# Writing the low halves of streamed weights over the loaded unit: six shared slots in place of four double ones, and a ScalarE lead of four or five units

## The reference, cut to what matters

```python
def swiglu(h, w1, w3, w2):
    return (jax.nn.silu(h @ w1) * (h @ w3)) @ w2

def conv_glu_ffn(x, w_up, conv_w, conv_b, w_down):
    h = causal_depthwise_conv(x @ w_up, conv_w, conv_b)
    g, u = jnp.split(h, 2, axis=-1)
    return (jax.nn.silu(g) * u) @ w_down
```

## Time and profile before

| | us |
|---|---|
| median of 3 runs | 2924.38 |
| lowest and highest | 2919.39, 2924.88 |
| the profiled execution | 2921.18 |
| its span, first to last instruction | 2919.4 |
| TensorE busy in it | 2652.9 |
| GpSimd busy in it | 1870.5 |
| ScalarE, DVE busy in it | 1460.7, 1122.1 |
| loaded from memory | 418.52 MB, 144 GB/s over the span |

### The profile page before, as it was taken

The page is one execution under the profiler, slowest core; times in us unless marked ns, Lnnn a source line. Parts: engine busy times, 40 slices in busy tenths (PEclk is TensorE's granted clock), DMA queues, the critical chain, the costliest instruction groups (busy, mean ns, idle before and its releaser), DMA issues.

```text
span 2919.4 us, 53645 instructions
## 1 busy us (share of the span) xinstructions
PE 2652.9 (91%) x19652; PEld 2493.6 (85%) x19652; DVE 1122.1 (38%) x2614; ACT 1460.7 (50%) x2539; POOL 1870.5 (64%) x789
## 2 busy tenths in 40 slices
PE   4999889999989989998889978899898899888997
PEld 2887679999977789998889977799878799878997
DVE  3316644111145621225343365433433433463334
ACT  4326644434444544445555565555545555464555
POOL 6437646878855678873468855388635588535686
PEclk8999999999999999999999998999979999999999
DMA  6224434555533545542345533255423355423454
GB/s 241 92 80 159 145 109 138 186 165 185 183 126 134 173 158 180 188 152 76 101 150 179 192 118 120 89 181 180 146 79 116 109 184 181 133 73 116 147 180 135
DMA packets 115063, 421.75 MB, mean 144 GB/s; under 512 B 12768, under 2 KB 13792, under 8 KB 114400
## 3 DMA queue, kind: packets, MB, share of 16 engines
q1 hardware_dynamic: 114336, 413.39, 42.7%
q10 hardware_dynamic: 576, 6.23, 0.5%
HBM read 418.52 MB, written 1.05 MB: 144 GB/s over the span
## 4 chain that ended last, share of the span: by engine, by line
PE 46%; issue 30%; POOL 17%; DVE 3%; ACT 2%; POOLq 0%; DMA 0%; ACTq 0%; SPq 0%; DVEq 0%
POOL ring_low L2064 17%; PE bank L560 8%; PE bank L561 8%; PE bank L566 8%; PE bank L551 6%; PE bank L552 6%; PE bank L553 5%; PE bank L767 1%; ACT scr L1188 1%; PE bank L796 1%; PE bank L684 1%; ACT ring_high L1078 1%; DVE rstd L1544 1%; PE bank L681 0%; DVE scr L1523 0%
## 5 line engine op out<-in xcount | busy, mean ns | idle before, releaser
L2064 POOL TENSOR_TENSOR ring_low<-ring,ring_high 128x1024 fp32r<-128x1024 f32 x785 | 1870.3, 2405 | 1028.7 <-ACT ring_high L1078 702.9
L560 PE MATMUL bank<-high,ring_high 128*128 128x256 f32 (+1 forms) x3372 | 858.5, 290 | 20.8 <-ACT ring_high L1294 10.0
L561 PE MATMUL bank<-low,ring_high 128*128 128x256 f32 (+1 forms) x3372 | 850.8, 288 | 0.0
L560 PEld LDWEIGHTS bank<-high,ring_high 128*128 128x128 f32 x3372 | 648.2, 192 | 29.6 <-ACT ring_high L1294 11.4
L561 PEld LDWEIGHTS bank<-low,ring_high 128*128 128x128 f32 x3372 | 648.4, 192 | 6.4
L1294 ACT ACTIVATE ring_high<-ring 128x1024 fp32r<-128x1024 f32 x462 | 479.7, 1052 | 54.1 <-PE bank L560 34.3
L566 PE MATMUL bank<-high,ring_low 128*128 128x256 f32 (+1 forms) x3372 | 492.6, 288 | 2.3 <-POOL ring_low L2064 2.3
L566 PEld LDWEIGHTS bank<-high,ring_low 128*128 128x128 f32 x3372 | 445.5, 192 | 9.5 <-POOL ring_low L2064 3.9
L1078 ACT ACTIVATE ring_high<-ring 128x1024 fp32r<-128x1024 f32 x323 | 337.9, 1055 | 166.0 <-PE bank L560 55.4
L551 PE MATMUL bank<-hid_high,ring_high 128*128 128x256 f32 x1232 | 352.1, 286 | 12.0 <-POOL ring_low L2064 12.0
L552 PE MATMUL bank<-hid_low,ring_high 128*128 128x256 f32 x1232 | 351.4, 285 | 0.0
(11 more groups left out here) (201 smaller groups left out, 3447.0 us busy)
## 6 DMA issues: line engine op xcount, KB each, us to landing
ring<-in_units SPq DMA_DIRECT2D x785, 512.0 KB, 3.3
xt<-in_x ACTq DMA_DIRECT2D x1, 2048.0 KB, 14.3
nbias<-in_bias ACTq DMA_DIRECT2D x1, 1536.0 KB, 7.8
consts<-in_consts ACTq DMA_DIRECT2D x1, 1472.0 KB, 8.5
vt<-in_mem ACTq DMA_DIRECT2D x1, 1024.0 KB, 6.3
out_x<-xt SPq DMA_DIRECT2D x8, 128.0 KB, 1.7
cols<-in_cols SPq DMA_DIRECT2D x1, 711.0 KB, 8.3
```

The source lines that it names most:

```text
L560: first = pe.matmul(out, w[0], x[0], start=start, stop=False)
L561: pe.matmul(out, w[0], x[1], start=False, stop=False)
L2064: pool.tensor_tensor(whole(ring_low, u), whole(ring, u), whole(ring_high, u).bitcast(fp32), ALU.subtract).then_inc(unit_ready, 1)
```

## The change

The low half is written over the unit that was loaded: `ring_low` becomes a second name, with the rounded type, for the memory of `ring`. The memory that is freed gives both rings six slots, of two blocks each (raw or low, and high). A slot can now be loaded again only when TensorE has released it, so SP waits for `unit_used` of unit u - 6, and ScalarE needs no wait of its own for a release. Outside the feed-forward stages `feed(u)` still goes up to u + 3. A feed-forward stage begins with `feed(u0, 5)`: units 3 and 4 are rounded before tile 0, and each tile rounds 3n + 4, 3n + 5 and 3n + 6. The last tiles leave out what brings the lead back to three units for the next stage.

```diff
-RING = 4
+RING = 6
+AHEAD = 4
...
+        ring_at = nc.sbuf_base
         ring = sb("ring", RING * UNIT)
+        ring_low = nc.alloc_sbuf_tensor_at("ring_low", [P, RING * UNIT], fp32r, offset=ring_at)
         ring_high = sb("ring_high", RING * UNIT, fp32r)
-        ring_low = sb("ring_low", RING * UNIT, fp32r)
...
-                        sp.wait_ge(unit_ready, r * RING + (s + 1 - RING))
+                        sp.wait_ge(unit_used, r * RING + (s + 1 - RING))
...
-                def feed(u):
+                def feed(u, ahead=AHEAD):
-                    while fed[0] < min(u + RING, N_UNITS):
+                    while fed[0] < min(u + ahead, N_UNITS):
                         v = fed[0]
                         act.wait_ge(loaded[v % RING], 16 * (v // RING + 1))
-                        if v >= RING:
-                            act.wait_ge(unit_used, v - RING + 1)
                         act.activation(whole(ring_high, v), whole(ring, v), ACT.Copy).then_inc(unit_high, 1)
...
-                    assert fed[0] == u0 + RING - 1
-                    def tile(r, n):
+                    assert fed[0] == u0 + AHEAD - 1
+                    feed(u0, AHEAD + 1)
+                    def tile(r, n, fed_ahead=False):
...
-                                act.wait_ge(unit_used, r * (3 * BODY) + (u - RING + 1))
...
-                            feed_tile([3])
+                            if not fed_ahead:
+                                feed_tile([4])
...
-                        feed_tile([4])
+                        feed_tile([5])
...
-                        feed_tile([5])
+                        if n < FT - 1:
+                            feed_tile([6])
                     for n in range(2):
-                        tile(0, n)
+                        tile(0, n, fed_ahead=n == 0)
...
-                    fed[0] = u0 + 3 * FT + 3
+                    fed[0] = u0 + 3 * FT + AHEAD - 1
```

More of the change, by code:

```diff
@@ L521, in _ @@
                 for u in range(rounds * RING, N_UNITS):
-                    sp.wait_ge(unit_ready, u + 1 - RING)
+                    sp.wait_ge(unit_used, u + 1 - RING)
                     sp.dma_start(whole(ring, u), stream[u]).then_inc(loaded[u % RING], 16)
```

## The result

The changed kernel took 2902.18 us (median of 4 runs, 2900.97 to 2904.37) beside 2924.09 us for the kernel before on the same chip: a ratio of 0.9929 (95% interval 0.9912 to 0.9946). It is faster, by 22 us (0.7%) where 31 were forecast, and lies inside the range of 2881 to 2910. The profiled execution took 2902.06 us with a span of 2900.3 us; the span of before was 2919.4, so 19.1 us are to be accounted for between the two traces. The low half is now line L2067, projections start at L553 and L562 (L551 and L560 before), and the low hidden half is L1818.

The account below looks back on a forecast made before the run. TensorE, 91% busy, was taken as the bound, with recoverable waits for late weights mostly at feed-forward starts. Terms 10.4 + 3.5 + 4.3 + 4.2 + 6.4 + 1.4 = 30.2 us gave 2893 us, range 2881 to 2910.

Parts of the forecast that it names:

- The starts of f0 to f3: Four feed-forward starts: units 3 and 4 rounded early let TensorE resume 2.6 us sooner each, 10.4 us in all.
- about 1.6 us: Sign of being right: at f0 to f3 one TensorE gap this long, ended by the low hidden half at L1815.
- x1, c0, memory: Feed-forward stages x1 and c0, and the memory's keys and values: earlier units save 3.5, 4.3 and 1.4 us.
- x0: Feed-forward stage that also modulates the context: 4.2 us gained, 3.4 at its first stall and 0.8 at its second.
- 2 or less: Sign of being right: TensorE's waits of L551 on the low half L2064 fall from 13.8 us to this.
- Clock behind the starts: After the starts of x0, f1, f2, f3: no fall to half clock, 1.6 us each, 6.4 us in all.
- In place, loads: Low halves written over their input stay at 2.40 us; loads waiting for TensorE's release of unit v - 6 cost nothing.
- Removed waits of ScalarE outside these stages: ScalarE no longer waits for TensorE's release; in conditioning between -3 and +3 us, taken as 0.
- The upper one: Rival at the feed-forward starts: stalls go, but the clock still falls or loads are late; 2897 to 2910, chance 0.24.
- GpSimd slower: Rival: in-place low halves on GpSimd take longer, gain gone at 2.94 us; above 2930 us, chance 0.08.
- DVE blocked: Rival: moved low halves block DVE in normalisations, 34 us, 2927; within little effect, 2911 to 2930, chance 0.10 together.
- does nothing: Rival: starts wait for hidden values, not weights; some 6 us gained, 2917, or zero, 2924; within little effect, chance 0.10.

Follow-up runs that it names:

- the repeat: The changed kernel once more, unedited: 2898.93 us, 0.9903 of the kernel before.
- its repeat: The kernel before once more, unedited: 2922.99 us.
- order alone: The kernel before, four slots and separate low-half buffers kept, with unit 3 rounded ahead of the stage's first evacuation: 2896.88 us, 0.9915.
- slots alone: The changed kernel without its early units, so unit 3 comes in tile 0 as before; six slots and in-place low halves kept: 2918.75 us, 0.9993.
- unit 3 alone: The changed kernel, six slots, with only unit 3 rounded ahead of tile 0 and unit 4 inside it: 2902.43 us, 0.9950.
- before with the delay: The kernel before with 20 overwritten matmuls (2.4 us) at the head of the latent attention's key up-projection: 2913.14 us, 0.9969.

## Why the prediction was right, and where it was not

**The starts of f0 to f3.** Forecast 2.6 us each. Measured 7.34 - 4.77 = 2.57 at all four, with one gap of 1.57 us ended by L1818 where "about 1.6 us" ended by L1815 was named. f0 as a whole gained only 1.8: the block ahead of the start took 0.8 us longer, with 10.2 us of half clock behind the root of its normalisation where there were 6.8. In the repeat it is 6.8 again.

**x1, c0, memory.** x1 gave 4.1 us for 3.5, and c0 4.4 for 4.3. The memory gave 2.1 for 1.4, but not for the reason given: 1.5 of it is clock, 3.4 us at 0.50 in both profiles of the kernel before (from 1239.0 in the first) that none of the other eleven has, in a place no term names. Of the two waits only the second (0.46) is gone, with 0.7 us in all. The first is still there, behind another engine:

```profile
1264.63 0.36 PE L553 MATMUL bank<-ring_high,high 128*128 128x256 f32 x1 [0.67 <-DVE nbias L1475]
```

The low half had hidden it: before, DVE's copy at this place (L1472 there) ended at 1278.07 us and the low half at 1278.11; with the low half early TensorE still waits for the copy. So this term came to half of its 1.4 us.

**x0.** The first stall went, the clock held (1.6), but the second stall did not shrink by 0.8: 1.36 us became 0.61 + 1.48. With them the waits of L553 on a low half are 2.3 us, over the "2 or less" that was named. The forecast let two low halves go ahead of the modulation and left out that the later ones meet the modulation elsewhere. Three L1565 took 1.27 us with GpSimd idle and 6.24 us with it at work, 4.72 before. The rule of the Trainium skill ("SBUF — State Buffer", "Who interferes with whom"), that a DVE instruction with two SBUF inputs contends with a GpSimd instruction that reads SBUF, agrees with that. As a rival (low halves caught in the 14 normalisation chains, 2927 us) it did not come: TensorE's waits on L1609 are 73.7 us in 10 places, 74.0 before.

**Clock behind the starts.** Forecast 1.6 us each for x0, f1, f2, f3, called a near thing. No half clock followed any of them. From unit 4 to the rounding of tile 2's hidden values f1, f2 and f3 take 12.96, 12.95 and 13.32 us, 14.41, 14.44 and 14.72 before: 1.4 to 1.5 each. How firm is that? The six profiles of kernels whose weights come late at the starts (before and its repeat, order alone, slots alone, unit 3 alone, before with the delay) have the fall behind f1 six times, behind f2 and f3 five times each, behind x0 twice; the seven with the changed order have none in 28 places. For f1 to f3 it is the change's gain, though the delayed kernel before loses the falls of f2 and f3 without it; x0's fall is in both profiles of the kernel before and in none of the other four, so its 1.6 us aren't shown to hang on late weights.

**In place, loads.** In place: 2408 ns for 2402, as taken. The Trainium skill ("GPSIMD Engine Reference", "2.1 Instruction dispatch") lays the cost of a two-input operation on its two inputs sharing one read port; the forecast's conclusion from it, that the target doesn't count, agrees with these numbers. Loads behind TensorE's release: no wait for a rounded half at any start.

**What failed.** The step "Removed waits of ScalarE outside these stages: between -3 and +3 us; I take 0", and with it the unstated one that whatever lies between the stages keeps its own time when it is moved. The conditioning (+1.1) is within the bound, and in the repeats the changed kernel is 0.2 us ahead at that root (436.6 for 436.8): no loss is shown there. The last attention (+4.8) and, in that execution, the first (+3.5) lie outside any term. The last was not slowed by weights, waits or loads: up to the fall its work and waits match to 0.01 us. It came at another moment, and TensorE fell to half clock behind a wait of 1.16 us behind which it had stayed up, for 17.1 us instead of the 3.4 that came later. In all 13 profiles the waits up to there are the same to a few hundredths; four have the 17.1 us, the shifted kernel before among them, eight the 3.4, one 6.8. The forecast had asked for the clock only where the change removes gaps. As these runs measure it, it should have carried for the attentions a bound of 5 us in both directions, and for the latent one a gain of up to 11 us, since its 23.9 us could only go.

**The rivals.** The upper one (2897 to 2910, 0.24) names the interval in which the result fell, for another reason: the clock took back 8 us, though not behind the starts. The forecast itself, 2883 to 2896, was missed; the 22 us are the sum of a mechanism that held and of half clock that nobody had counted. "GpSimd slower", "DVE blocked" and "does nothing" are refuted by L2067, L1609 and the missing L1294.

**Open.** Why the same matmuls behind the same waits run at full clock in one profile and at half in another, and for 3.4, 6.8, 10.2, 13.7, 17.1 or 23.9 us. The runs show that the work itself doesn't decide, and that shifting it changes the outcome; with one profile of each kernel they don't part the moment cleanly from the chance of the execution, and they give no rule by which a new kernel's stretches could be foretold. Why some executions of one kernel lie 14 us from the others is open too, beyond the granted clock that goes with it.

## What to carry to other kernels

Round ahead in idle time as far as the slots allow, and count the lead in the stage where the consumer releases units in blocks: here one more unit early was worth 9 us and the second, which needed the slots, 17. A wait that ends on one engine can hide one on another at the same place: price it only when the second is known. When a change shifts a kernel whose TensorE sits near a clock change, compare stage by stage, not by total: a total can be 11 us off for a stage that nobody touched. Where a half-clock stretch is long, try a delay of a few matmuls ahead of it before any redesign, and judge it by several executions with their granted clocks, since stretches also come and go by themselves.

## What the runs showed of the hardware that was not expected

- In the latent attention half clock behind a wait of 0.98 us is all or nothing: 23.9 us in eight of the 13 profiles, none in five, for the same instructions; a delay of about 1.2 us removed it as wholly as one of 2.4 us, and the stage was 8.3 to 9.6 us shorter. The other two attentions have lengths between: 3.4, 6.8 or 17.1 us in the last, none to 13.7 us in the first.
- 32 score matmuls took 13.06 us with the fall and 8.39 us without; the stage 11.2 us more.
- Writing over an input cost GpSimd next to nothing: 2408 ns at the median against 2402 for 128x1024.
- Added work made the fastest kernel: 23 matmuls more, 2887.43 us.
- Executions of one kernel can lie 14 us apart, with mean granted clocks of 0.958 to 0.959 and 0.965 (unit 3 alone early: 2915.03 and 2917.04, 2899.42 to 2903.47).
